# Step order, places of the memory projections and probability buffers in a three-pass projection network

## The reference

```
q = (rmsnorm(q_lat, q_norm_g) @ w_uq);  kv = (rmsnorm(kv_lat, kv_norm_g) @ w_ukv)
y = attn.reshape(B, T, MLA_WIDTH) * silu(gate)
uc = conv4(u);  r, i = sigmoid(blocks(uc) @ w_rg + b_rg), sigmoid(blocks(uc) @ w_ig + b_ig)
a = exp(-8 * r * softplus(-lam));  hs = scan(a, sqrt(1 - a * a) * i * uc)
kv = rmsnorm(mem, mem_norm) @ w_mem_kv          # one for each layer of the second block
w = softmax(q1 k1) - lam * softmax(q2 k2);  o = rmsnorm(w @ v, subln)
x = x + concat(o_self, o_mem) @ w_out;  x = x + square(relu(rmsnorm(x) @ w_up)) @ w_down
```

## Time and profile before

| | |
|---|---|
| median of 3 runs | 934.82 us (934.51 to 935.3) |
| profiled execution | 939.73 us, span from first to last instruction 937.9 |
| TensorE busy | 867.1 us, mean granted clock 0.96 |
| VectorE, ScalarE busy | 587.4 and 542.3 us |
| DMA packets | 137.40 MB, mean 146 GB/s |

### The profile page before, as it was taken

One profiled execution on the slowest core, in us unless ns is written; L12 is line 12 of the kernel. 1 busy time (PEld: TensorE's weight loads), 2 busy tenths in 40 slices (PEclk: granted clock), 3 DMA queues, 4 the chain that ended last, 5 costly groups with the idle time before them and its releaser, 6 DMA issues.

```text
span 937.9 us, 16231 instructions
## 1 busy us (share of the span) xinstructions
PE 867.1 (92%) x6638; PEld 822.7 (88%) x6638; DVE 587.4 (63%) x1055; ACT 542.3 (58%) x953; POOL 2.6 (0%) x6
## 2 busy tenths in 40 slices
PE   6999999988879987989999999899988899999995
PEld 6897779988878787889999999887868899999995
DVE  6995656787876686466646464844763666455643
ACT  7754775679765657655535353646673555454532
POOL 0000000000000000000000000000000000000001
PEclk9998999999888999989999999989998999999997
DMA  8553324445352344354666666533332455666521
GB/s 305 168 160 110 113 68 133 137 143 164 115 186 90 91 129 142 124 169 148 190 181 185 187 190 180 180 114 90 102 109 85 151 175 188 182 184 189 189 70 45
DMA packets 41449, 137.40 MB, mean 146 GB/s; under 512 B 4384, under 2 KB 8736, under 8 KB 41376
## 3 DMA queue, kind: packets, MB, share of 16 engines
q1 hardware_dynamic: 41376, 136.37, 47.3%
HBM read 135.31 MB, written 1.05 MB: 145 GB/s over the span
## 4 chain that ended last, share of the span: by engine, by line
PE 81%; DVE 9%; ACT 6%; issue 2%; DMA 0%; DVEq 0%; ACTq 0%; SPq 0%
PE bank L663 22%; PE bank L665 22%; PE bank L664 22%; DVE weights_lo L1420 2%; PE bank L934 2%; PE bank L668 2%; ACT weights_hi L1011 2%; DVE arena L1420 2%; PE bank L669 2%; PE bank L670 2%; PE bank L887 1%; PE bank L886 1%; DVE temp L1420 1%; DVE operand_lo L1426 1%; ACT arena L1011 1%
## 5 line engine op out<-in xcount | busy, mean ns | idle before, releaser
L663 PE MATMUL bank<-operand_hi,weights_hi 128*128 128x256 f32 (+1 forms) x1860 | 539.8, 290 | 24.7 <-DVE weights_lo L1420 14.2
L664 PE MATMUL bank<-operand_lo,weights_hi 128*128 128x256 f32 (+1 forms) x1860 | 536.3, 288 | 0.0
L665 PE MATMUL bank<-operand_hi,weights_lo 128*128 128x256 f32 (+1 forms) x1860 | 535.9, 288 | 0.0
L1011 ACT ACTIVATE weights_hi<-weights_raw 128x1024 fp32r<-128x1024 f32 (+2 forms) x254 | 264.7, 1045 | 290.1 <-PE bank L665 281.1
L1420 DVE TENSOR_TENSOR weights_lo<-weights_raw,weights_hi 128x1024 fp32r<-128x1024 f32 (+2 forms) x254 | 305.5, 1208 | 186.7 <-ACT weights_hi L1011 186.3
L663 PEld LDWEIGHTS bank<-operand_hi,weights_hi 128*128 128x128 f32 x1860 | 362.6, 195 | 30.8 <-DVE weights_lo L1420 14.9
L665 PEld LDWEIGHTS bank<-operand_hi,weights_lo 128*128 128x128 f32 x1860 | 362.9, 195 | 0.0
L664 PEld LDWEIGHTS bank<-operand_lo,weights_hi 128*128 128x128 f32 x1860 | 361.0, 194 | 0.0
L668 PE MATMUL bank<-weights_hi,operand_hi 128*128 128x256 f32 (+1 forms) x140 | 43.3, 309 | 0.0
L669 PE MATMUL bank<-weights_lo,operand_hi 128*128 128x256 f32 (+1 forms) x140 | 41.8, 299 | 0.0
L670 PE MATMUL bank<-weights_hi,operand_lo 128*128 128x256 f32 (+1 forms) x140 | 41.7, 298 | 0.0
(11 more groups left out here) (173 smaller groups left out, 688.0 us busy)
## 6 DMA issues: line engine op xcount, KB each, us to landing
weights_raw<-stream_dram SPq DMA_DIRECT2D x244, 512.0 KB, 4.2
weights_raw<-stream_dram SPq DMA_DIRECT2D x6, 384.0 KB, 3.5
residual<-xT_dram SPq DMA_DIRECT2D x4, 272.0 KB, 4.7
weights_raw<-stream_dram SPq DMA_DIRECT2D x4, 256.0 KB, 5.0
temp<-memT_dram SPq DMA_DIRECT2D x4, 256.0 KB, 5.5
arena<-memT_dram SPq DMA_DIRECT2D x4, 256.0 KB, 4.4
out_dram<-residual SPq DMA_DIRECT2D x3, 256.0 KB, 2.1
constants<-consts_dram SPq DMA_DIRECT2D x1, 536.0 KB, 7.9
```

The source lines that it names most:

```text
L663: e.matmul(to, w_h, x_h, start=start, stop=False, skip_group_check=True)
L664: e.matmul(to, w_h, x_l, start=False, stop=False, skip_group_check=True)
L665: return e.matmul(to, w_l, x_h, start=False, stop=stop, skip_group_check=True)
L1011: return e.activation(to, of, ACT.Copy, bias=0.0, **scale)
```

## The change

The 252 units stay the same; their order changes. Gate units 10 and 11 come before a_uq; the layer-0 memory projections move from the MLA stage between b_in's units and the gates units; those of layer 1 move from the attention of layer 0 to the end of b_in; in layers 0 and 1 of the second block v2 and in2 swap places, and out2 goes through all its first halves (k0 = 0), then its second. The latents are multiplied by their norm's row before they are split, by a new step on DVE (latent_norm), so queries, keys and values are copied on ACT without a factor; one pair of rope rows is made instead of two. The heads get slots by hand, heads 4 to 7 of the MLA behind the last gate unit; mean and spread of in2 and up come one unit later. Memory heads and layer 1 use four probability buffers. Some banks and operand buffers change. All times of TIMES are new; the diff shows those that the steps below name.

```diff
     halves("a_in", 0, 0)
-    rows_of("a_in", 0, range(2, 10))
-    for pair_, gate in (((0, 8), 10), ((2, 10), 11), ((4, 6), None)):
-        units.extend(Unit("a_uq", 0, 0, 3, m, 2) for m in pair_)
-        rows_of("a_in", 0, [gate] if gate else [])
+    rows_of("a_in", 0, range(2, 12))
+    units.extend(Unit("a_uq", 0, 0, 3, m, 2) for m in (0, 8, 2, 10, 4, 6))
     units.extend(Unit("a_k", 0, 0, 2, m, 4) for m in (0, 4))
     units.extend(Unit("a_v", 0, 0, 2, m, 4) for m in (8, 12))
     rows_of("a_in", 0, (12, 13))
-    rows_of("mem_k", 0, range(2))
-    halves("mem_v", 0, 2)
     rows_of("a_out", 0, range(8))
-    rows_of("b_in", 0, range(6))
-    units.extend(Unit("gates", 0, 0, 4, m, 2) for m in (0, 1))
+    rows_of("b_in", 0, range(3))
+    rows_of("mem_k", 0, (0,))
+    rows_of("b_in", 0, (3,))
+    rows_of("mem_k", 0, (1,))
+    rows_of("b_in", 0, (4, 5))
+    units.append(Unit("mem_v", 0, 0, 4, 2, 2))
+    units.append(Unit("gates", 0, 0, 4, 0, 2))
+    units.append(Unit("mem_v", 0, 4, 4, 2, 2))
+    units.append(Unit("gates", 0, 0, 4, 1, 2))
     rows_of("b_in", 0, (6, 7, 8, 9))
-    units.extend(Unit("gates", 0, 4, 4, m, 2) for m in (0, 1))
-    rows_of("b_in", 0, range(10, 16))
+    units.append(Unit("gates", 0, 4, 4, 0, 2))
+    rows_of("b_in", 0, (10,))
+    units.append(Unit("gates", 0, 4, 4, 1, 2))
+    rows_of("b_in", 0, (11, 12, 13))
+    rows_of("mem_k", 1, range(2))
+    rows_of("b_in", 0, (14, 15))
+    halves("mem_v", 1, 2)
     units.extend(Unit("b_out", 0, k0, 4, m, 2) for k0, m in HALVES)
     for layer in range(2):
         halves("in2", layer, 18)
         rows_of("in2", layer, (0, 1, 6, 7))
         halves("v2", layer, 12)
-        rows_of("in2", layer, (2, 3, 8, 9, 4, 5, 10, 11))
+        rows_of("in2", layer, (2, 3, 8, 9))
         halves("v2", layer, 14)
+        rows_of("in2", layer, (4, 5, 10, 11))
         halves("v2", layer, 16)
-        if layer == 0:
-            rows_of("mem_k", 1, range(2))
-            halves("mem_v", 1, 2)
-        units.extend(Unit("out2", layer, k0, 4, m, 2) for k0, m in HALVES)
+        units.extend(Unit("out2", layer, k0, 4, m, 2) for k0 in (0, 4) for m in (0, 2, 4, 6))
...
     if w.kind == "a_in":
         return "" if w.m0 < 2 and w.k0 == 0 else "vsf" if w.m0 < 5 else "vs"
     if w.kind == "a_uq":
-        return "vs" if w.m0 >= 8 else "v"
+        return "vs" if w.m0 >= 8 else "s"
...
-        return "v" if w.kind == "a_k" else "vsf"
+        return "s" if w.kind == "a_k" else "vsf"
...
 TIMES = {
...
+    ("scalar", "sub_scale"): (92.1, 93.71),
...
+    ("vector", "softmax_first"): (74.09, 74.18, 74.55, 74.73, 76.5, 78.5, 79.8, 79.2, 83.33, 83.67, 84.2, 84.6,
+        88.62, 88.75, 88.88, 89.5, 164.8, 165.17, 165.33, 165.67, 169.75, 169.5, 171.17, 170.8, 173.33, 173.67,
+        176.2, 176.4, 181.33, 181.67, 182.33, 182.67),
...
+        48.6, 54.33, 54.67, 58.29, 58.14, 60.08, 65.5, 68.67, 70.14, 70.43, 73.5, 74.82, 75.67, 80.5, 81.5, 88.12,
...
+        88.38, 97.1, 97.2, 97.4, 97.7, 101.67, 101.33, 106.5, 110.75, 109.67, 113.5, 115.33, 121.5, 124.67, 131.5,
...
+        134.33, 134.67, 142.33, 140.67, 150.5, 152.33, 156.5, 160.2, 160.8, 162.67, 164.6, 167.8, 169.25, 171.33,
...
     a = AT["a_in", 0, 0, 0]
     statistics(a + 3, "a")
-    vector("rope_rows_a", "k")
+    vector("rope_rows_a")
     hold(a + 5.06, range(a + 1, a + 5))
     statistics(a + 7, "q")
     statistics(a + 7, "kv")
-    vector("rope_rows_a", "q")
+    for m in range(5):
+        vector("latent_norm", m)
+        scalar("latent_hi", m)
+        vector("latent_rest", m)
...
     first = AT["a_k", 0, 0, 0]
-    for h in range(HEADS):
-        s = first + h
-        tensor(s + 0.91, "mla_scores", h)
+    for h, (at, turned, valued) in enumerate(((0, 2, 3), (1, 3, 4), (2, 4, 5), (3, 5, 5.1), (4, 5.1, 5.15), (5, 5.15, 5.2),
+                                              (5.1, 5.2, 5.25), (5.15, 5.25, 5.3))):
+        at, turned, valued = first + at + 0.5, first + turned + 0.52, first + valued + 0.54
+        tensor(at, "mla_scores", h)
         vector("mla_mask", h)
...
-        tensor(s + 1.93, "mla_turn", h)
+        tensor(turned, "mla_turn", h)
         scalar("mla_turned", h)
-        tensor(s + 2.95, "mla_values", h)
+        tensor(valued, "mla_values", h)
...
-    mem = AT["mem_k", 0, 0, 0]
     for i in range(4):
         scalar("memory", 0, i)
         vector("memory", 0, i)
-    statistics(mem, "mem")
-    hold(mem + 2.05, [mem + 1])
+    statistics(first + 11, "mem")
 
     b = AT["b_in", 0, 0, 0]
     statistics(b, "b")
...
+    for i in range(4):
+        scalar("memory", 1, i)
+        vector("memory", 1, i)
     last = LAST["b_in", 0]
     for m in range(8):
         vector("scan", m)
...
         scalar("y_b", m)
         vector("y_b_rest", m)
 
-    def head(layer, kind, h, s, at):
-
-        tensor(s + 0.91, "scores", layer, kind, h)
+    def head(layer, kind, h, scored, turned, valued):
+
+        tensor(scored + 0.91, "scores", layer, kind, h)
...
-        tensor(s + 1.93, "turn", layer, kind, h)
+        tensor(turned + 0.93, "turn", layer, kind, h)
         scalar("turned", layer, kind, h)
-        tensor(at + 0.96, "values", layer, kind, h)
+        tensor(valued + 0.96, "values", layer, kind, h)
...
-    def diff_head(h, s, at):
+    def diff_head(h, scored, turned, valued):
         for c in range(2):
-            tensor(s + 0.91, "scores", 0, "diff", 2 * h + c)
+            tensor(scored + 0.91, "scores", 0, "diff", 2 * h + c)
...
-        tensor(s + 1.93, "turn", 0, "diff", h)
+        tensor(turned + 0.93, "turn", 0, "diff", h)
         scalar("turned", 0, "diff", h)
-        tensor(at + 0.96, "diff_values", h)
+        tensor(valued + 0.96, "diff_values", h)
         scalar("diff_out", h)
 
     for layer in range(2):
         i = AT["in2", layer, 0, 18]
-        statistics(i, f"in2_{layer}")
+        statistics(i + 1, f"in2_{layer}")
         vector("rope_rows_2", layer)
-        hold(i + 2.06, [i + 1])
+        hold(i + 3.06, [i + 1])
         for h in range(MEM_HEADS):
-            head(layer, "mem", h, i + 3 + h, i + 5 + h)
+            head(layer, "mem", h, i + 3 + h // 2, i + 6 + h // 2, i + 8 + h // 2)
         if layer == 0:
             vector("scale_x")
-            for h, (s, at) in enumerate(((7, 9), (8, 10), (12, 18), (13, 18), (16, 20), (17, 20))):
-                diff_head(h, i + s, i + at)
-            for group, t in enumerate((i + 19.5, i + 21.3)):
+            for h, slots in enumerate(((7, 9, 11), (8, 10, 12), (12, 14, 15), (13, 15, 16), (18, 20, 21), (18, 20, 21))):
+                diff_head(h, *(i + n for n in slots))
+            for group, t in enumerate((i + 17.3, i + 22.1)):
                 vector("sub_mean", group)
                 scalar("sub_root", group)
                 vector("sub_norm", group)
                 scalar("sub_scale", group)
-            for h in range(0, DIFF_HEADS, 2):
-                tensor(i + 23.9, "sub_turn", h)
+            for h, n in ((0, 18), (2, 19), (4, 23)):
+                tensor(i + n + 0.97, "sub_turn", h)
                 scalar("sub_turn", h)
                 vector("sub_turn", h)
-            for k in range(4):
-                scalar("memory", 1, k)
-                vector("memory", 1, k)
         else:
-            places = ((7, 9), (8, 10), (9, 11), (10, 12), (12, 18), (13, 18), (14, 18), (15, 18), (16, 19), (17, 19),
-                      (18, 19), (18, 19))
-            for h, (s, at) in enumerate(places):
-                head(1, "moba", h, i + s, i + at)
+            for h, slots in enumerate(((8, 10, 12), (8, 10, 12), (9, 11, 13), (9, 11, 13),
+                                       (12, 14, 16), (12, 14, 16), (13, 15, 17), (13, 15, 17),
+                                       (18, 20, 21), (18, 20, 21), (19, 21, 22), (19, 21, 22))):
+                head(1, "moba", h, *(i + n for n in slots))
         u = AT["up", layer, 0, 0]
-        statistics(u, f"mlp_{layer}")
-        hold(u + 2.05, [u + 1])
+        statistics(u + 1, f"mlp_{layer}")
+        hold(u + 3.05, [u + 1])
...
         def memory_tile(layer, i):
-            return temp[5 + i % 2][:, 0:512] if layer == 0 else region(7680 + 512 * (i % 2), 512)
+            return temp[(5, 6, 4, 6)[2 * layer + i % 2]][:, 0:512]
 
 
...
                 return [w.m0 // 2]
             if w.kind == "up":
-                return [4 + (w.m0 // 2) % 3]
+                return [(5, 6, 4)[(w.m0 // 2) % 3]]
             if w.kind == "a_in" and w.m0 < 2:
                 return [0, 1]
-            if w.kind == "a_in" and w.m0 < 10:
+            if w.kind == "a_in" and w.m0 < 12:
                 return [w.m0 % 6]
             if w.kind == "a_uq":
-                i = {0: 10, 8: 12, 2: 15, 10: 17, 4: 20, 6: 22}[w.m0]
+                i = 2 * (0, 8, 2, 10, 4, 6).index(w.m0)
                 return [i % 6, (i + 1) % 6]
-            if w.kind == "a_in" and w.m0 < 12:
-                return [{10: 14, 11: 19}[w.m0] % 6]
...
```

(47 more changed lines are left out.)

226 lines of the change are left out of this document (112 added, 114 removed), and 32 rows, old and new, of the table TIMES.

## The result

| | before | after |
|---|---|---|
| median | 934.66 us (932.23 to 935.3) | 848.8 us (848.12 to 850.07) |
| ratio, 95% interval | | 0.9087 (0.9068 to 0.9107) |
| profiled execution, span | 939.73, 937.9 us | 850.07, 847.9 us |
| TensorE busy, mean granted clock | 867.1 us, 0.96 | 822.8 us, 0.994 |
| VectorE, ScalarE busy | 587.4, 542.3 us | 569.1, 532.4 us |

The forecast was 884 us with a range of 866 to 905. Lines 672 to 674 are 663 to 665 of before, 1447 is 1420, 943 is 934, 865 is 856.

A forecast was written before the change was run, and what follows sets the result against it. TensorE was taken as the bound, with unchanged work, so only its losses could move: 83.8 us (idle plus clock) in ten stretches would fall to 32.7. The saving of 51.1 from 934.8 gave 884 us, range 866 to 905.

The forecast's parts named there:

- By my walk some 8 us: Latents: row, product, copy and rest take some 8 us, covered by three units (9 us); loss 3.5 becomes 0.5.
- the chain fits: Start of in2, layer 0: 4.8 us from last add to mean fits under 5.7 us of work; 11.7 becomes 3.
- gates 3: Gates and b_in: units between the gates units cover waits for banks held by sigmoids; loss 7.2 becomes 3 us.
- attention of layer 1 6.8: Attention of layer 1, which has no sub-norm: loss 15.3 becomes 6.8 us, bounds 3 and 13.
- second rival: Covers half fail: splits held behind heads' steps, six slips of 4.5 us bring 27 us back, 911 us; chance 0.22.
- row of 68.9: MLA heads' stretch before (68.9 to 146.6 us), source of the slip price: 1.19 us idle and 3.3 of clock.
- Attention of layer 0: Waits around sub_turn and out2, 5 us, plus 5 for lower clock and departed memory units; 15.0 becomes 10.
- MLA: MLA heads: memory units leave, the wait before the first scores goes; loss 6.5 becomes 4 us, bounds 1 and 12.
- rule on function switches: ScalarE in the MLA: the skill's 2.66 us per switch against 1.30 in the trace would add 1.4 us each.
- Starts: Starts of in2 and MLP: layer 0 11.7 to 3 and 6.6 to 0.8, layer 1 6.3 to 1.8 and 5.0 to 0.8.
- All covers hold: First rival: every part at its lower bound, 10.5 us left, 73 saved, 862 us; chance 0.10 (under 870).
- slower rival: Third rival: inside the MLPs TensorE waits for banks or hidden tiles at 32 pairs, 112 us more, 996; chance 0.04.

The follow-up runs named there:

- e1: Changed kernel with odd head's steps no longer right behind the even head's in seven slots: 859.0 us, ratio 0.9174 to the kernel before.
- e5: Kernel before with values steps of heads 0 to 3 (memory in both layers, blockwise in layer 1) put together in twos: 931.9 us, ratio 0.9939.
- e9: Changed kernel with VectorE's split done twice for six units whose margin was small: 855.2 us, ratio 0.9152 to the kernel before.
- after_again: The changed kernel as it is, run once more as reference: 850.3 us, ratio 0.9095 to the kernel before.
- e2: Changed kernel with mean and spread of in2 and up one unit earlier, as in the kernel before: 861.8 us, ratio 0.9203.
- e4: Changed kernel with the banks of up in the old order 4, 5, 6: 853.1 us, ratio 0.9127 to the kernel before.
- e6: Kernel before with only VectorE's and ScalarE's lists at the four in2 and up starts placed as in the changed kernel: 923.0 us, ratio 0.9861.
- e7: Kernel before with only mean and spread of in2 and up one unit later: 927.9 us, ratio 0.9902.
- e8: Kernel before with the edits of e6 and e7 together: 918.9 us, ratio 0.9808.
- e11: Changed kernel with the two gates units of each half adjacent again, the memory and b_in units behind them: 854.3 us, ratio 0.9134.
- e16: Changed kernel with scores of MLA heads 2 to 7 issued in twos at the even head's slot, rope products adjacent: 844.7 us, ratio 0.9010.

## Why the prediction was wrong in size

TensorE was the bound, and what it had lost was won back in the ten stretches named. But "Only what TensorE loses can move" was wrong: its work became shorter too. The 85.9 us are 34.8 more than the 51.1 forecast: 24.3 because less was left in the stretches, some 10 to 11 from the overlap of heads, the rest small. Point by point:

- **Overlap of heads: a missing term.** "The change gives it the same 252 weight units and the same attention steps" took equal counts for equal time. 10 to 11 us by the groups; e1 takes such overlap away in seven slots (7.8 to 9.5 us), e5 gives it to six pairs of the kernel before (5.7). It could have been read in the slots of the diff, which put heads h and h + 1 at one time, and in the trace of before, where two late blockwise heads already stood together.
- **What is left: 8.4 us instead of 32.7.** The step that failed is the tax on covers whose sum I had found to fit. "By my walk some 8 us" under 9 gave 0.5, found 0; "the chain fits" gave 3, found 0.7; gates 3 and b_out 2, found 0; attention of layer 1 6.8, found 0.1. Four finds lie below their lower bounds (gates 1, b_out 0.5, in2 start 1, layer 1's attention 3). e9 shows both halves of the error: a margin of 0.05 us was enough, and a slip costs about 1 us. The 4.5 us of the second rival, with 3.3 us of clock from the row of 68.9, was the price of a rare case.
- **Attention of layer 0: right place, half the size.** 10 forecast, 4.7 found, 1.7 of it at the out2 unit behind the last sub_turn, 1.6 at the scores of the last differential heads. The 5 us "for what the lower clock makes of them" did not come: the clock is 1.00 over the stretch with 4.7 us idle in it.
- **MLA: 4 forecast, 2.8 found**, 1.8 of them the lower clock at the end of the stage. The prediction named a lower clock in the MLA tail as a sign that it was wrong; it came there, 0.64 over 123.8 to 128.4 us, but in after_again, the same kernel, it did not. The rule on function switches did not bite: the load of 1.28 us at 121.23 is followed by the silu at 122.53, 1.30 us in all, as before.
- **Starts.** The cause (order in the lists, bank of the first up unit, one more unit of cover) was right, and e2, e4, e6 and e7 price it: 10.5 and 3.4 us in the changed kernel, 13.0 and 9.2 in the one before. e8 shows that the terms don't add: in the old slots a part of the gain turns into waits of the heads' turns.
- **Recurrence.** The fillers at the gates units are worth 4.0 us (e11), most of it at one wait; the layer-0 keys and layer-1 units were not tried apart, nor were the new order of the latents and that of out2, so for these stretches the cause is argued from the lists, not shown.
- **Rivals.** "All covers hold" had 0.10 and is what happened: its 862 us less 11.0 for the overlap would have been 851. The slower rival, banks inside the MLPs, did not come: TensorE is busy 170.5 of 170.5 us from 378.7 to 549.2.
- The profiled execution of before stood 4.9 us above its median, that of after 1.3: 3.6 of the 90.0 us between the spans are this, not the change.

Of the signs named beforehand the mean of in2 (a wait of 0.31 us), the first up units (at once), the clock over latents and MLP starts (1.00) and the gates (no 2 us wait) came as said; "about 10 us in attention of layer 0" did not.

## What to carry to other kernels

When steps only change places, ask first which of them become neighbours: here two heads' matmuls on different 64-row halves of the array (scores, into two banks) or on different 64-column halves (values, into one bank), issued back to back, took the time of one, and a single step of another shape between them took that away. When the walk through the queues says that a cover fits, cost it at nothing and put the doubt in the range; price a slip by what is missing, and the lower clock behind a wait of about 1 us as an extra that may not come (it did not in e9). A stall that is removed is worth its full length only if the next step in line, here the heads' turns, is moved too.

## What the runs showed of the hardware

Products of two heads on rows 0 to 63 and 64 to 127 run at once: 8 matmuls in 1.14 us against 4 in 1.13, 12 rope products in 1.12 us against 2.16 for 12 full ones of equal columns. So do values of two heads on 64 output partitions each, though both write bank 7: 4 matmuls in 0.66 us against 2 in 0.65. In e1 scores steps (64 rows) and values steps (128 rows, 64 columns) alternate, and the scores step still takes 0.85 us from start to start (583.91 to 584.76), as alone in the kernel before (644.95 to 645.80). The Trainium skill, TensorEngine Tiling (Array Packing), section Key Properties, says that a change of tiling mode drains the engine, and no row here shows a cost beyond what a lone step has; a lone step also stands between steps of another shape, so what the change costs in itself can't be read here.

The lower clock is not tied to a wait of a given length. The changed kernel was granted 1.00 over 67.7 to 75.8 us, behind a wait of 0.49 us; e1 has the same wait and was granted 0.81 over 67.0 to 76.0. Behind the last values step (0.53 us of wait before it in all three) the next unit ran at 0.64 in the changed kernel and at 1.00 in e16 and in after_again, which is the changed kernel once more. What decides it stays open. The unit in the changed kernel, then in after_again:

```profile
123.80:128.40 4.60, 4.60 (x27) 4.60 (x27) 3.93 (x6) 1.38 (x2) 0.00 (x0) 0.64 0.93 298
```

```profile
124.10:128.70 4.60, 4.60 (x39) 4.60 (x38) 4.09 (x8) 2.58 (x4) 0.00 (x0) 1.00 0.82 284
```
